# Attention over pairs of heads: the second head's turns moved ahead of the first head's values, its copy given to ScalarE

## What is computed

```python
def attend(blk):
    qn, qr = blk
    s = jnp.einsum('bqhd,bkhd->bhqk', qn, k_nope) + jnp.einsum('bqhr,bkr->bhqk', qr, k_rope)
    p = jax.nn.softmax(s.astype(jnp.float32) * scale, axis=-1)
    return jnp.einsum('bhqk,bkhd->bqhd', p.astype(v.dtype), v)
```

## Time and profile before

| | us |
|---|---|
| median of 3 runs | 1644.21 |
| lowest and highest of them | 1641.92, 1649.26 |
| the profiled execution, its own time | 1647.26 |
| span in its trace | 1645.3 |
| the attention block, first to last instruction | about 564 to 777 |
| TensorE's granted clock, mean over the span | 0.951 |

### The profile page before, as it was taken

How to read it: one execution, slowest core, us unless ns; L and a number is a source line. 1 busy time by engine, 2 the same in 40 slices (tenths; PEclk the granted TensorE clock), 3 DMA queues, 4 the chain that set the end, 5 groups by cost and what they waited for, 6 DMA issues and landing times. The chain is left out here.

```text
span 1645.3 us, 19694 instructions
## 1 busy us (share of the span) xinstructions
PE 1472.4 (89%) x7275; PEld 814.4 (49%) x7276; DVE 570.4 (35%) x1134; ACT 354.9 (22%) x735; POOL 97.3 (6%) x96
## 2 busy tenths in 40 slices
PE   5999999958859899998999539999999999999968
PEld 2555544437748655665455334444444444444423
DVE  1122136545647633433677640111101111111017
ACT  2122122135524333343211101101111011110111
POOL 0000010000000000000000000111111111111000
PEclk8999999979989999999999759999999999999979
DMA  9201011126640200000411159987898889999936
GB/s 377 91 26 39 0 8 40 40 81 202 198 138 1 101 2 0 0 0 17 160 64 52 51 213 424 367 309 295 321 410 320 316 364 368 422 368 411 410 143 279
DMA packets 98181, 305.49 MB, mean 186 GB/s; under 512 B 18065, under 2 KB 53053, under 8 KB 88920
## 3 DMA queue, kind: packets, MB, share of 16 engines
q1 hardware_dynamic: 89880, 287.08, 45.1%
q0 software_dynamic: 8064, 16.80, 2.8%
q10 hardware_dynamic: 192, 1.03, 0.2%
HBM read 289.86 MB, written 25.76 MB: 192 GB/s over the span
## 5 line engine op out<-in xcount | busy, mean ns | idle before, releaser
L384 PE MATMUL ps<-w_in_tok,uT 128*128 128x512 f32 (+2 forms) x512 | 190.3, 532 | 1.9 <-ACT uT L316 1.9
L1677 PE MATMUL ps<-w_gate_sb,x_slotsT 128*128 x320 | 144.5, 605 | 9.7 <-issue 9.7
L1693 PE MATMUL ps<-w_down_sb,hidT 128*128 x320 | 148.0, 605 | 0.0
L384 PEld LDWEIGHTS ps<-w_in_tok,uT 128*128 128x128 f32 x512 | 97.3, 191 | 89.4 <-issue 58.8
L1677 PE MATMUL ps<-w_up_sb,x_slotsT 128*128 x320 | 140.6, 592 | 0.0
L1881 DVE TENSOR_TENSOR hid<-silu_g,ps 128x512 f32<-128x512 f32 x20 | 13.8, 688 | 294.9 <-PE ps L1677 294.9
L1388 PE MATMUL ps<-uT,hT 128*128 128x512 f32 x256 | 114.4, 601 | 0.0
L519 PE MATMUL ps<-uT,mod 128*128 128x512 f32 x256 | 111.0, 593 | 0.8 <-PEq L203 0.8
L1677 PEld LDWEIGHTS ps<-w_gate_sb,x_slotsT 128*128 128x128 f32 x320 | 59.9, 192 | 87.0 <-issue 87.0
L1677 PEld LDWEIGHTS ps<-w_up_sb,x_slotsT 128*128 128x128 f32 x320 | 60.8, 190 | 76.5 <-issue 76.5
L1693 PEld LDWEIGHTS ps<-w_down_sb,hidT 128*128 128x128 f32 x320 | 57.5, 189 | 66.5 <-issue 65.6
(11 more groups left out here) (374 smaller groups left out, 1841.6 us busy)
## 6 DMA issues: line engine op xcount, KB each, us to landing
light_gate_sb<-in_w_gate SPq DMA_DIRECT2D x20, 2048.0 KB
light_up_sb<-in_w_up SPq DMA_DIRECT2D x20, 2048.0 KB
light_down_sb<-in_w_down SPq DMA_DIRECT2D x20, 2048.0 KB
w_gate_sb<-in_w_gate SPq DMA_DIRECT2D x12, 2048.0 KB
w_up_sb<-in_w_up SPq DMA_DIRECT2D x12, 2048.0 KB, 15.3
w_down_sb<-in_w_down SPq DMA_DIRECT2D x12, 2048.0 KB
mod<-in_w_ada SPq DMA_DIRECT2D x8, 1024.0 KB, 9.4
w_ada_late<-in_w_ada SPq DMA_DIRECT2D x8, 1024.0 KB, 9.5
```

The lines of the kernel that those rows point to most:

```text
L384: mm = nc.tensor.matmul(ps[:, 2 + g, 0:n], self.uT[:, k, t * P:(t + 1) * P], wt[:, k, c0:c0 + n], start=k == 0, stop=k == KD - 1)
L1677: m = m_.matmul(ps[:, bank, :], xT[:, k, :], wt[:, bass.ds(buf, 1), k, :].rearrange("p a f -> p (a f)"), start=k == 0, stop=k == KD - 1)
L1693: m = m_.matmul(ps[:, 5 + half, :], hT[:, k, :], wd[:, bass.ds(buf, 1), k, half * 512:half * 512 + 512].rearrange("p a f -> p (a f)"), sta ...
```

## The change

TensorE: `turn(1)` moves from behind `out` of head 0 to the place ahead of it. It now waits until both engines have read head 0's turned probabilities out of banks 4 and 5. `out` loses its two waits for copies; ahead of `out` of head 1 stands a wait for ScalarE's copy alone. ScalarE: for head 1 it copies both banks in one instruction of 1024 columns, behind a wait on `s_o`. VectorE: its copy for head 1 goes; `s_td` now counts one copy for each pair.

```diff
                 def out(n, h):
                     j = h % 2
-                    pe.wait_ge(s_td, n + 1)
-                    pe.wait_ge(s_ta, n + 1)
                     pe.wait_ge(s_oe, n + 1)
...
                         pe.wait_ge(s_p, n + 2)
                         scores(1 - g)
+                        pe.wait_ge(s_td, t * 2 + g + 1)
+                        pe.wait_ge(s_ta, n + 1)
+                        turn(1)
                         out(n, 2 * g)
-                        turn(1)
+                        pe.wait_ge(s_ta, n + 2)
                         out(n + 1, 2 * g + 1)
...
                 def turned(n, j):
+
                     act.wait_ge(s_t, n + 1)
-                    a.copy(pT[:, j, 4:8, :], ps[:, 5, :].rearrange("p (k t) -> p k t", k=4)).then_inc(s_ta, 1)
+                    if j == 0:
+                        a.copy(pT[:, 0, 4:8, :], ps[:, 5, :].rearrange("p (k t) -> p k t", k=4)).then_inc(s_ta, 1)
+                    else:
+                        act.wait_ge(s_o, n)
+                        a.copy(pT[:, 1].rearrange("p k t -> p (k t)"), ps[:, 4:6, :].rearrange("p a b -> p (a b)")).then_inc(s_ta, 1)
...
-                def turned(n, j):
+                def turned(n):
+
                     dve.wait_ge(s_t, n + 1)
-                    v.tensor_copy(pT[:, j, 0:4, :], ps[:, 4, :].rearrange("p (k t) -> p k t", k=4)).then_inc(s_td, 1)
+                    v.tensor_copy(pT[:, 0, 0:4, :], ps[:, 4, :].rearrange("p (k t) -> p k t", k=4)).then_inc(s_td, 1)
...
-                        turned(n, 0)
+                        turned(n)
...
                         out(n, t, 2 * g)
-                        turned(n + 1, 1)
                         out(n + 1, t, 2 * g + 1)
```

## The result

The changed kernel takes 1651.91 us (median of 16 runs, 1647.87 to 1656.6) where the kernel before takes 1644.62 (16 runs). The ratio of their times is 1.0037, 95% interval 1.0025 to 1.005: slower by some 6 us (4 to 8), clear of noise but small. The medians lie 7.3 us apart, inside that interval. One of the 16 runs of the kernel before took 3309.3 us, and no profile shows it; without it the median is 1644.21.

A forecast was written before the change was run, and what follows sets the result against it. TensorE's sequence was taken to bound the block, with the copy wholly in its path: 4.0 us over 16 pairs plus 1.5 us at 7 loop ends, 5.5 us in all, gave 1649.7 us; range 1642.5 to 1656.

The forecast's parts named there:

- The order costs nothing by itself, and could cover a copy: TensorE, turn(1) ahead of out of head 0: no added cost, and cover for a copy of about 1 us.
- The stretch of 4.07 us: Scores' end to out of head 1, with ScalarE's copy in TensorE's path: 4.07 us instead of 3.82, 0.25 longer a pair.
- The 4.0 us: Slowdown forecast from the longer stretch before out of head 1: 16 × 0.25 us.
- The copy's price: ScalarE's 1024-column copy for head 1, absent from the trace before, was to take 1.02 us.
- The rival with two one-bank copies' length: Between the heads' outputs, copy 1.17 us and handover 0.16: 9.3 us slower in total, 1653.5; chance 0.20.
- The loop's end: From out of head 1 to turn(0): 2.52 us instead of 2.30, at 7 loop ends, 1.5 us.
- The total: Whole kernel: 4.0 + 1.5 = 5.5 us slower, 1649.7 us against the median.
- The clock: Rival: longer TensorE gaps lower its granted clock in the scores, 49 us more, 1698; chance 0.02.
- The early copy: Rival: the s_o wait is met early, the copy hides under out of head 0; 19.6 us faster, 1624.6; chance 0.05.

The follow-up runs named there:

- another version: Changed kernel with each engine copying half for head 1, ScalarE's wait on s_o kept ahead of its 512-column copy: 1643.07 us, 0.9992 of the kernel before.
- the order alone: Changed kernel with each engine copying half for head 1 and no wait on s_o, turn(1) still first: 1622.6 us, 0.9852 of the kernel before.

## Why the prediction was right

The whole of it hung on one reading of the code, that the new wait asks for the first head's output of the same pair. The runs bear this out from three sides: without the wait, or with the same wait asking for one output less, the gap is gone (22.19 and 22.18 us a loop turn instead of 25.44); with the copy doubled, the gap grows by the whole second copy; with the wait put back on another version, that version's gain is gone. Point by point:

- **The order costs nothing by itself, and could cover a copy.** Right. No gap stands ahead of `turn(1)` in the changed kernel, and the order alone gives 22 us.
- **The stretch of 4.07 us.** From the scores' end (`turn(1)` at 632.00) to the second head's values at 636.04 it is 4.04. The terms: `turn(1)` 0.93 instead of 0.88; the values of the first head 1.95 to their modelled end instead of 2.05; handover 0.10 instead of 0.07; copy 1.01 instead of 1.02; handover back 0.05. The errors cancel, and that is luck. The first two have one source, which the sum overlooked: what stands first behind the scores takes a little longer. Before, these were the values (2.05); now they are the turns (1.09 where they had 1.04), and the values behind the turns take 1.95. The 4.0 us became 16 × 0.22 = 3.5.
- **The copy's price.** The groups of the changed kernel have it:

```profile
L1214 ACT COPY probsT<-ps 128x1024 f32<-128x1024 f32 x16 | 16.2, 1012 | 75.7 <-PE ps L1175 75.7
...
L1211 ACT COPY probsT<-ps 128x512 f32<-128x512 f32 x16 | 9.4, 585 | 7.1 <-PE ps L1168 6.5
```

  1012 ns, against 1.02 us worked out from the slope between 256 and 512 columns. (1012 − 585) / 512 is 0.834 ns a column. By the Trainium skill, *ScalarE: Activation LUTs*, section "What ACT_TABLE_LOAD costs", an ACTIVATE with immediate scale and bias takes 186 ns plus 0.833 ns a column. The trace agrees on the slope, and its fixed part, 585 − 427 = 158 ns, is 28 ns smaller. The rival with two one-bank copies' length is out.
- **The loop's end.** `out` of head 1 to `turn(0)` was to go from 2.30 to 2.52; it is 650.80 − 648.28 = 2.52.
- **The total.** 5.5 us forecast; 5.1 us by the loop turns, 6 (4 to 8) by the times. The median of 1651.91 lies 2.2 above the forecast's 1649.7, 0.4 of it since the kernel before has 1644.62 over more runs.
- **The clock.** 1.00 from 590 to 770 us with gaps of 1.16, as with 0.90. That rival did not come. With gaps of 2.07, in the doubled copy behind its wait, the clock did fall at some of them.
- **The early copy.** Its price of 19.6 us was near what the kernel without the wait shows: 8 × (24.80 − 22.19) = 20.9 by its loop turns, 21 by its time. Here too errors cancel in part. In the pair inside the loop turn the unbroken values run 0.21 us closer than the rival's two of 1.89, and `turn(1)` costs 0.93 instead of 0.88 in both pairs; at the loop's end the two values take 3.79, where the rival had 3.78.
- Off was the price of the short gap with the doubled copy, an experiment's expectation and not the forecast.

## What to carry to other kernels

When a wait is added that is to order a copy behind earlier readers, write down the semaphore's value at which the last real reader is done, with its start value and the argument as the callee sees it (`turned(n + 1, 1)` passes a number that is already one higher), and compare it with the value waited for: an excess of one is correct, silent, and here turned a gain of 21 us into a loss of 6. Look also at whether an earlier wait orders the same thing already. The kernel before has no wait on `s_o` ahead of this copy: it waits for the second head's turns alone, which stand behind the last reader of the old `pT[:, 1]` in TensorE's own order, in the changed kernel too. A reorder that is to hide work shows its success in one place of the trace, the start of the hidden work: if that stands behind the cover's end instead of under it, look there before anywhere else. And price the move of work between engines apart from the reorder: two engines with 512 columns each were better than one with 1024, in either order.

## What was not expected of the hardware

- **A short pause costs more than its length.** Without a pause, both heads' values together take 633.43 − 629.86 = 3.57 us to the next turn, 0.21 less than two of 1.89. The doubled copy without the wait has a pause of 0.23 between them, and takes 639.79 − 635.72 = 4.07 us, 0.50 more. The rows show where the rest lies: unbroken, the 32 records last 3.74 us; broken in two, they last 1.95 + 2.05 = 4.00, and 0.26 + 0.23 is 0.49. Record by record, they start 0.11 us apart and last 0.28 each by their modelled ends, so that the last one before a pause runs out uncovered, 0.17 us; and the first one behind a pause takes 0.38, 0.10 longer. These are the trace's records; what the engine does in that time they don't show.
- **The block's head varies.** The first scores took 6.74 us in the run before and 5.40 in that without the wait, and the second scores 4.84 where the runs before and after had 5.40. No instruction up to the first of these differs, so 1 to 2 us of a comparison between two traces can lie there. The long form, 6.6 to 6.8 us, also came in the changed kernel, in both kernels with the order alone (with and without the wait) and in the doubled copy without the wait; the other experiments had 5.4. From the first scores of the kernel without the wait:

```profile
566.39 5.40 PE L1158 MATMUL ps<-knT,qs_tile 128*128 128x512 f32 x8 [3.65 <-ACT qrs_tile L1200]
...
577.87 4.84 PE L1158 MATMUL ps<-knT,qs_tile 128*128 128x512 f32 x8
```

It is the granted clock that differs: its mean is 0.54 over the 6.74 us of the run before, 0.68 over these 5.40, 0.75 over the 4.84, and 1.00 where such a stretch takes 3.60 or 3.70.
